# Conv mixer's tokens in phase order written by the norm ahead, and the channel norm's factor and bias moved into the silu

## The reference, cut to what matters

```python
def conformer_conv_mixer(h, w_in, b_in, dw, dw_b, ln_g, ln_b, w_out, b_out):
    a, gate = jnp.split(h @ w_in + b_in, 2, axis=-1)
    u = a * jax.nn.sigmoid(gate)                         # GLU, (B,S,D)
    u = depthwise_causal_conv(u, dw, width=31) + dw_b
    u = jax.nn.silu(layer_norm(u, ln_g, ln_b))           # over the channels
    return u @ w_out + b_out
for layer in range(2):
    h = h + 0.5 * swiglu_ffn(rms_norm(h, g), w_in, w_out)       # D_FF = 2816
    h = h + mixer[layer](rms_norm(h, g))
    h = h + memory_cross_attention(rms_norm(h, g), mem_n, wq, wkv, wo)
    h = h + 0.5 * swiglu_ffn(rms_norm(h, g), w_in, w_out)
y = rms_norm(h, final_norm)
```

## Time and profile before

| | us |
|---|---|
| median of 3 runs | 6055.49 (6054.27 to 6544.5) |
| profiled execution, device time | 6057.36 |
| its span on the slowest core (3) | 6055.7 |
| spans of the 8 cores | 6045.7 to 6055.7 |
| granted TensorE clock, mean | 0.986 to 0.987 |
| PE busy on that core | 5838.7 (96%) |
| DVE, ACT, POOL busy | 2989.5, 2245.4, 629.6 |

### The profile page before, as it was taken

The page is one execution under the profiler, slowest core; times in us unless marked ns, Lnnn a source line. Parts: engine busy times, 40 slices in busy tenths (PEclk is TensorE's granted clock), DMA queues, the critical chain, the costliest instruction groups (busy, mean ns, idle before and its releaser), DMA issues.

```text
span 6055.7 us, 91272 instructions; the slowest of 8 cores (6045.7 to 6055.7 us)
## 1 busy us (share of the span) xinstructions
PE 5838.7 (96%) x32113; PEld 2815.8 (46%) x32113; DVE 2989.5 (49%) x4244; ACT 2245.4 (37%) x3810; POOL 629.6 (10%) x700
## 2 busy tenths in 40 slices
PE   7999998999999998999989999899999999989999
PEld 3555554444444443444444445544444444445444
DVE  5444556643534523754364355564445344266435
ACT  4213888511311304641151158972123112266113
POOL 1100442000000000000000014400000000000000
PEclk9999999999999999999999999999999999989999
DMA  7665322322322022133352212224223202123221
GB/s 140 100 100 89 40 31 51 45 37 30 53 31 30 11 39 39 47 53 42 42 146 39 27 25 22 27 46 60 36 35 52 29 11 36 25 63 47 35 32 56
DMA packets 388456, 287.50 MB, mean 47 GB/s; under 512 B 111337, under 2 KB 344849, under 8 KB 385968
## 3 DMA queue, kind: packets, MB, share of 16 engines
q0 software_dynamic: 342192, 195.13, 25.2%
q1 hardware_dynamic: 45824, 86.55, 4.6%
HBM read 428.49 MB, written 33.55 MB: 76 GB/s over the span
## 4 chain that ended last, share of the span: by engine, by line
PE 91%; issue 2%; DVE 2%; ACT 2%; POOL 1%; DMA 1%; SPq 0%; DVEq 0%; ACTq 0%; POOLq 0%
PE ps L662 40%; PE ps L677 20%; PE ps L897 8%; PE ps L827 4%; PE ps L808 4%; PE ps L1050 3%; PE ps L577 2%; PE ps L1139 2%; PE ps L1002 2%; PE ps L925 2%; PE ps L1071 1%; PE ps L737 1%; PE ps L992 1%; DVE hn_tok L573 1%; PE ps L822 0%
## 5 line engine op out<-in xcount | busy, mean ns | idle before, releaser
L662 PE MATMUL ps<-arena 128*128 128x512 bf16 x11264 | 2487.5, 380 | 5.3 <-ACT arena L579 4.6
L662 PEld LDWEIGHTS ps<-arena 128*128 128x128 bf16 x11264 | 1098.8, 98 | 1314.2 <-issue 19.3
L664 ACT ACTIVATE arena<-ps 128x512 bf16<-128x512 f32 x704 | 419.7, 596 | 2584.3 <-PE ps L662 2573.6
L665 DVE TENSOR_TENSOR arena<-ps,arena 128x512 bf16<-128x512 f32 x704 | 486.8, 692 | 1768.2 <-PE ps L662 1751.1
L677 PE MATMUL ps<-arena 128*128 128x512 bf16 x5632 | 1248.5, 379 | 0.3 <-DVE h L679 0.3
L679 DVE SCALAR_TENSOR_TENSOR h<-ps,h 128x512 f32<-128x512 f32 x1536 | 1042.9, 690 | 213.1 <-PE ps L677 207.5
L677 PEld LDWEIGHTS ps<-arena 128*128 128x128 bf16 x5632 | 551.0, 98 | 663.9 <-issue 1.9
L897 PE MATMUL ps<-arena 128*128 128x512 bf16 x1024 | 468.0, 631 | 0.0
L604 POOL DMA_DIRECT2D arena<-ffn_w_in x176 | 154.6, 881 | 2426.7 <-PE ps L662 1729.1
L549 ACT ACTIVATE junk<-h 128x1024 bf16<-128x1024 f32 x288 | 303.8, 1055 | 233.7 <-DVE h L679 120.3
L1050 PE MATMUL ps<-arena 128*128 128x512 bf16 x1536 | 381.6, 387 | 0.0
(11 more groups left out here) (162 smaller groups left out, 4560.9 us busy)
## 6 DMA issues: line engine op xcount, KB each, us to landing
arena<-ffn_w_in POOLq DMA_DIRECT2D x176, 512.0 KB, 8.4
arena<-ffn_w_out POOLq DMA_DIRECT2D x88, 512.0 KB, 8.3
arena<-hgrn_w_in POOLq DMA_DIRECT2D x64, 256.0 KB, 5.4
y<-arena SPq DMA_DIRECT2D x32, 512.0 KB, 2.7
h<-x SPq DMA_DIRECT2D x20, 512.0 KB, 6.5
arena<-xattn_wkv POOLq DMA_DIRECT2D x16, 512.0 KB, 10.1
folded_a<-arena SPq DMA_DIRECT2D x16, 512.0 KB, 10.0
folded_v<-arena SPq DMA_DIRECT2D x16, 512.0 KB, 10.2
```

Of the source, the lines that this page charges most:

```text
L662: P.op("pe", lambda e, bb=bb, ga=ga, k=k, j=j: e.matmul(psb(bb), lhsT=wiv[:, ga, k, j * 128:(j + 1) * 128], rhs=hnT[:, k, blk * 512:(blk + ...
L664: P.op("act", lambda e, bg=bg, j=j: e.activation(out=sg[j].ap, in_=psb(bg), func=AF.Silu), reads=psk(bg), writes=sg[j].keys())
L665: P.op("dve", lambda e, bu=bu, j=j, q=q: e.tensor_tensor(out=actv[:, q, :], in0=psb(bu), in1=sg[j].ap, op=ALU.mult), reads=psk(bu) + sg[j] ...
```

## The change

- `norm_block` gets `phased`. For the conv mixer it multiplies each 128x128 piece of `hn_tok` with `phase`, a permuted identity, in place of the transpose: two PSUM banks and two ACT copies of 512 fp32 values a tile in place of one bank and one copy of 1024 bf16 values. `hnT` then lies in phase order, and `glu` reads 512 elements side by side.
- The channel norm's gain and bias are brought as columns into `vecs`, which has one value per partition. Where DVE made two passes and ACT a silu over each quarter, DVE makes one pass (minus mean, times 1/deviation, bf16 out), and the silu is taken as the results of the `spread` matmuls are copied out, all eight on ACT, with the factor and the bias of each channel. The broadcast loads of gain and bias are gone.
- At the end of a sequence `tail` also emits the norm of the next sequence's block `blk - 1`; the staging buffers of the final norm are four in place of two.
- The first FFN of each sequence begins with a pair of groups. In the first one `x` tiles 4 to 7 go through SP's queue, the second group's weights are loaded ahead of them, the loads of the folding steps wait for the last `x` tile ("tick"), and the steps lie at other packs.

```diff
+        phase = sb("phase", [128, 128], BF16)
...
+        P.op("pool", lambda e: e.tensor_copy(out=phase[:].rearrange("p (q s) -> p q s", q=4), in_=ident[:].rearrange("p (s q) -> p q s", q=4)), reads=["ident"], writes=["phase"])
...
-        def norm_block(blk, g, skip_rstd=False):
+        def norm_block(blk, g, skip_rstd=False, phased=False):
             if not skip_rstd:
                 block_rstd(blk)
             for tt in range(blk * 4, blk * 4 + 4):
                 s = tt % 2
                 P.op("dve", lambda e, tt=tt, s=s: e.scalar_tensor_tensor(out=hn_tok[:, s, :], in0=h[:, tt, :], scalar=stat[:, 2, tt:tt + 1], in1=gB[:, g, :], op0=ALU.mult, op1=ALU.mult),
                      reads=[("h", tt), ("rstd", blk), ("gB", g)], writes=[("hn_tok", s)])
+                if phased:
+                    part = hnT[:, :, blk * 512:(blk + 1) * 512].rearrange("p c (q f s) -> p c q f s", q=4, f=4)[:, :, :, tt % 4, :]
+                    for c0 in (0, 4):
+                        b = P.bank()
+                        for c in range(4):
+                            P.op("pe", lambda e, c=c, c0=c0, s=s, b=b: e.matmul(ps[:, P.place[b], c * 128:(c + 1) * 128], lhsT=hn_tok[:, s, (c0 + c) * 128:(c0 + c + 1) * 128], rhs=phase[:], start=True, stop=True),
+                                 reads=[("hn_tok", s), "phase"], writes=psk(b))
+                        P.op("act", lambda e, c0=c0, b=b, part=part: e.activation(out=part[:, c0:c0 + 4], in_=psb(b).rearrange("p (c q s) -> p c q s", c=4, q=4), func=AF.Copy), reads=psk(b), writes=hnT_keys(blk))
+                    continue
                 b = P.bank()
                 for c in range(KC):
                     P.op("pe", lambda e, c=c, s=s, b=b: e.transpose(out=psb16(b)[:, c * 128:(c + 1) * 128], in_=hn_tok[:, s, c * 128:(c + 1) * 128], identity=ident[:]),
                          reads=[("hn_tok", s), "ident"], writes=psk(b))
                 P.op("act", lambda e, tt=tt, b=b: e.activation(out=hnT[:, :, tt * 128:(tt + 1) * 128], in_=psb16(b).rearrange("p (c t) -> p c t", t=128), func=AF.Copy), reads=psk(b), writes=[k for c in range(KC) for k in hnT_buf.keys(c * T + tt * 128, c * T + (tt + 1) * 128)])
...
-        fin_stage = [ABuf(arena, ARENA_B - 8192 + i * 4096, D, F32) for i in range(2)]
+        fin_stage = [ABuf(arena, ARENA_B - 16384 + i * 4096, D, F32) for i in range(4)]
...
-                fs = fin_stage[fin_i[0] % 2]
+                fs = fin_stage[fin_i[0] % 4]
...
-            packs = [(0,)] + [(g, g + 1) for g in range(1, NG, 2)]
+            if which == 0 and layer == 0:
+                packs = [(0, 1), (2, 3), (4, 5), (6,), (7, 8), (9, 10)]
+            else:
+                packs = [(0,)] + [(g, g + 1) for g in range(1, NG, 2)]
             load_wi(0)
             if lead is not None:
-                lead(wi[base % NW].keys(0, KC * 256), wi[base % NW].keys(KC * 256, 2 * KC * 256), lambda: load_wo(0, [("landed", 0, 5)]))
+                load_wi(1)
+                lead(wi[base % NW].keys(0, KC * 256), wi[(base + 1) % NW].keys(0, KC * 256), lambda: load_wo(0, [("landed", 0, 5)]))
             else:
                 load_wo(0)
             for g in range(1, max(NW, NO)):
-                late = () if lead is None else [("landed", 0, (11, 13, 15, 15)[g - 1])]
-                if g < NW:
+                late = () if lead is None else [("landed", 0, (7, 13, 15, 15)[g - 1])]
+                if g < NW and (lead is None or g > 1):
                     load_wi(g, late)
                 if g < NO:
                     load_wo(g, late)
...
-                if middle is not None and i == 4:
+                if middle is not None and i == 2:
                     middle()
-                if steps and i >= 7:
+                if steps and i >= 4 and len(pack) == 2:
                     steps.pop(0)()
...
-                wload(wkv_[0], xa_wkv_d[l][:, hh * 256:(hh + 1) * 256].rearrange("(k p) n -> p k n", p=128), fw[0].keys())
-                wload(wkv_[1], xa_wq_d[l][:, hh * 256:(hh + 1) * 256].rearrange("(k p) n -> p k n", p=128), fw[1].keys())
+                wload(wkv_[0], xa_wkv_d[l][:, hh * 256:(hh + 1) * 256].rearrange("(k p) n -> p k n", p=128), fw[0].keys(), ["tick"])
+                wload(wkv_[1], xa_wq_d[l][:, hh * 256:(hh + 1) * 256].rearrange("(k p) n -> p k n", p=128), fw[1].keys(), ["tick"])
...
-            lnb = CV.take(D, F32)
...
                     ba = P.bank()
                     for (bb, a) in ((bg, 1), (ba, 0)):
                         for k in range(KC):
-                            P.op("pe", lambda e, bb=bb, a=a, k=k, v=v, blk=blk: e.matmul(psb(bb), lhsT=v[:, a, k, :], rhs=hnT[:, k, blk * 512:(blk + 1) * 512].rearrange("p (t q) -> p q t", q=4), start=(k == 0), stop=(k == KC - 1)),
+                            P.op("pe", lambda e, bb=bb, a=a, k=k, v=v, blk=blk: e.matmul(psb(bb), lhsT=v[:, a, k, :], rhs=hnT[:, k, blk * 512:(blk + 1) * 512], start=(k == 0), stop=(k == KC - 1)),
...
-            P.op("sp", lambda e: e.dma_start(out=lnb.ap, in_=cv_lnb_d[0].partition_broadcast(128)), writes=lnb.keys(), dma=True)
-            load_gain(ga, cv_lng_d[0])
             load_gain(gn, xa_norm_d[1])
             for b in range(NB):
...
                 for q in range(4):
                     a = b * 4 + q
                     uk = u2_keys(b, q, 0, D)
-                    P.op("dve", lambda e, b=b, q=q, a=a: e.scalar_tensor_tensor(out=u2v[:, b, q, :], in0=u2v[:, b, q, :], scalar=lst[:, 0, a:a + 1], in1=gB[:, ga, :], op0=ALU.subtract, op1=ALU.mult), reads=uk + [("lmean", b), ("gB", ga)], writes=uk)
-                    P.op("dve", lambda e, b=b, q=q, a=a: e.scalar_tensor_tensor(out=u2v[:, b, q, :], in0=u2v[:, b, q, :], scalar=lst[:, 5, a:a + 1], in1=lnb.ap, op0=ALU.mult, op1=ALU.add), reads=uk + lnb.keys() + [("lrs", b)], writes=uk)
                     yb = y_of(b, q)
-                    P.op("act", lambda e, b=b, q=q, yb=yb: e.activation(out=yb.ap, in_=u2v[:, b, q, :], func=AF.Silu), reads=uk, writes=yb.keys())
+                    P.op("dve", lambda e, b=b, q=q, a=a, yb=yb: e.tensor_scalar(out=yb.ap, in0=u2v[:, b, q, :], scalar1=lst[:, 0, a:a + 1], scalar2=lst[:, 5, a:a + 1], op0=ALU.subtract, op1=ALU.mult), reads=uk + [("lmean", b), ("lrs", b)], writes=yb.keys())
                 for c in range(KC):
                     bt = P.bank()
                     for q in range(4):
                         yb = y_of(b, q)
                         P.op("pe", lambda e, c=c, bt=bt, q=q, yb=yb: e.matmul(psb(bt), lhsT=yb.ap[:, c * 128:(c + 1) * 128], rhs=spread[:, q:q + 512], start=(q == 0), stop=(q == 3)), reads=yb.keys() + ["spread"], writes=psk(bt))
-                    if c % 2 == 0:
-                        P.op("act", lambda e, bt=bt, c=c, yTv=yTv: e.activation(out=yTv[:, c, :], in_=psb(bt), func=AF.Copy), reads=psk(bt) + ([("yT", b, 0)] if c else []), writes=[("yT", b, c)] + ([] if c else yk))
-                    else:
-                        P.op("dve", lambda e, bt=bt, c=c, yTv=yTv: e.tensor_copy(out=yTv[:, c, :], in_=psb(bt)), reads=psk(bt) + [("yT", b, 0)], writes=[("yT", b, c)])
+                    P.op("act", lambda e, bt=bt, c=c, yTv=yTv: e.activation(out=yTv[:, c, :], in_=psb(bt), func=AF.Silu, scale=vecs[:, V_LG, c:c + 1], bias=vecs[:, V_LO, c:c + 1]), reads=psk(bt) + [("vec", V_LG), ("vec", V_LO)] + ([("yT", b, 0)] if c else []), writes=[("yT", b, c)] + ([] if c else yk))
...
+        ahead = []
...
-                P.op("act", lambda e: e.activation(out=stat[0:1, 0, 18:19], in_=stat[0:1, 0, 0:1], func=AF.Copy), reads=[("ss", 0), ("h", 0)], writes=["tick"])
+                P.op("act", lambda e: e.activation(out=stat[0:1, 0, 18:19], in_=stat[0:1, 0, 0:1], func=AF.Copy), reads=[("ss", 0), ("h", 0), ("landed", 0, 15)], writes=["tick"])
...
+                    phased_at.add(len(seq_stages)) if layer == 1 else None
...
+                if sq_i + 1 < NSEQ:
+                    ahead.append(begin_norm(seq_stages[0][0]))
+
                 def tail(blk):
                     inner(blk)
+                    if sq_i + 1 < NSEQ and blk:
+                        norm_block(blk - 1, ahead[0])
...
-                g0 = begin_norm(seq_stages[0][0])
+                g0 = begin_norm(seq_stages[0][0]) if sq_i == 0 else ahead.pop()
                 def lead(k0, k1, then, g0=g0):
                     for tt in range(4, 8):
-                        load_x_tile(0, tt, "pool", k0 if tt < 6 else k1)
+                        load_x_tile(0, tt, "sp", k0)
                     norm_block(1, g0)
                     then()
                     for blk in range(2, NB):
                         for tt in range(blk * 4, blk * 4 + 4):
                             load_x_tile(0, tt, "pool", [("landed", 0, tt - 4)])
                         norm_block(blk, g0)
-                norm_block(0, g0)
-                if sq_i > 0:
-                    for blk in range(1, NB):
-                        norm_block(blk, g0)
+                norm_block(0 if sq_i == 0 else NB - 1, g0)
```

(11 more changed lines are left out.)

12 lines of the change are left out of this document (6 added, 6 removed).

## The result

The changed kernel took 5780.22, 5781.39, 6367.04 and 6465.86 us, with a median of 6074.22; the kernel before took 6054.27, 6055.49, 6332.73 and 6544.5, with a median of 6194.11 (the table of before has the three of them that were there then). In the two long runs of the changed kernel the cores of one die show a granted clock of 0.86 to 0.89 and the other die's cores spans of 5770 to 5783 us, so the comparison, and the times, ratios and means of the experiments, rest on runs and cores without this. The ratio to the kernel before is **0.9547 [0.9506, 0.9588]**, where the bracket is a 95% interval. The profiled execution took 5780.22 us, 277.1 less than the 6057.36 of before; the forecast's sum was 291.6.

What follows compares the result with a forecast made beforehand. PE was taken as the bound, with 91% of the chain of waits, losing time to slow glu matmuls and gaps. 241.6 - 4 + 20 + 22 + 12 = 291.6 us off 6057.4 gave 5765.8, stated as 5764 us; range 5736 to 5822.

Steps and rivals of the forecast that it cites:

- the median of the runs is 1.9 us below it: Last step: from the profiled execution's forecast of 5765.8 us to the median of the runs, 5764 us.
- Part 1: Conv mixer's glu: contiguous reads take a matmul from 452 to 216 ns, giving 241.6 us, less 4 us of new waits.
- for the first chunk 2 us a sequence: Glu's first chunk: the last block's norm has less glu to hide under; 4 us lost in all.
- Part 2: Norm in phase order: PE unchanged, ACT 5 us more in all, nothing on the path.
- Part 3: End of the conv mixer: one DVE pass and later silus give 10 us a sequence, 20 us; ends 4 and 30.
- PE's first output matmuls can pay 0 to 4 us for it: Conv mixer's end: eight silus in a row on ACT, 6.4 us, replace copies of 2.4 us and may delay PE.
- Rival 3: Seams fail through ACT's table order or norms holding up the last pack; sum 251 us, time 5805 us; chance 15%.
- Part 4: Change of sequence: norms emitted ahead and a paired first pack take back 22 of 28 us; ends 6 and 30.
- Part 5: Start: folding loads moved away and the second group's work put in PE's gap give 12 us; ends 3 and 18.
- the tiles land some 5 us earlier: Start: without the folding loads beside them the x tiles land sooner, while PE has 6.9 us of second-group matmuls.
- Sum: All terms together: 291.6 us off the profiled execution's 6057.4 us, which gives 5765.8 us.

Runs made afterwards that it cites:

- relay32: The changed kernel with the relayout issued as 32 DMAs of 16 channels in place of 16 of 32; 5932.63 us, one run.
- phase_alone: The kernel before with only the norm in phase order and glu's contiguous read; 5834.4 us in one run.
- rest_alone: The changed kernel with the plain norm and glu's read at a step of four set back; 6019.0 to 6022.4 us, ratio 0.9927.
- no_ahead: The changed kernel with the second sequence's norms emitted behind all final blocks, as before; 5808.96 us, one run.
- steps: The kernel before with eight read orders of the same 512 columns, one per conv mixer chunk; 216 to 918 ns a matmul.

## Why the prediction was right, and where not

The mechanism held for an execution of the kernel: 277 us against 291.6, and 5780 and 5781 us lie within 5736 to 5822. The stated time did not hold, since it stood for the median of the runs. By the steps:

- **From the sum to the median.** The step that failed is "the median of the runs is 1.9 us below it". The median of these four runs is 6074.22, 294.0 us above the profiled execution and outside the range, because two of them took 6367 and 6466 us. The sum took one execution's time for all and had no term for this, though a run of 6544.5 stood in the table of before. What makes an execution so long stays open.
- **Part 1.** The removed 241.6 measured 241.1 of PE's busy time. The new waits were put at 4 us, "for the first chunk 2 us a sequence", and came to about 9 (241.6 less the 232.6 of the account): 10.2 more in the first three chunks of both sequences, 1.3 less in the others. The sum took the steady queue of the earlier trace rows for the first chunks as well. The place of the relayout in a steady chunk was right to 0.2 us; relay32 showed that its slack is real and not large.
- **Part 2.** Zero was right: phase_alone's recurrences, conv end and change of sequence equal before's within 0.4 us. Its rest is 4.5 above, but rest_alone and no_ahead, from the same chip, have 2 to 4 more than the others too, and the kernel before took 8 us more there, so this seems to go with the chip.
- **Part 3.** 20 was forecast, 12.3 came. The step that failed is "PE's first output matmuls can pay 0 to 4 us for it": the gap's share was right (11.6 in one sequence, forecast 10.3 to 12.7), but PE pays nothing at the output matmuls. It pays 5.4 us a sequence at the attention's norm, where ACT's tables, 12 loads in place of 7, are changed between silu and root. Rival 3 named "silus behind ACT's table order" and gave it no price of its own. The DVE pass took 0.80 us, not the 1.28 that I took as its upper bound; the 32 spread matmuls took 9.03 us, not 6.92, at a granted clock of 0.78.
- **Part 4.** 22 was forecast, 27.6 came: nearly all of the 28 that I had counted, since the clock stayed up too. The reading that norms ahead and the pair are both needed held: either alone gives 8.5.
- **Part 5.** 12 was forecast, 6.5 came, less 2.7 in the recurrences. The step "the tiles land some 5 us earlier" and PE has the second group to do left out that this group's weights must land as early, over DMA engines without a free share: PE waits for them three times, 6.3 us.
- **Sum.** 5 + 8 + 5 + 3 less than forecast at parts 1, 3, 5 and the recurrences, 6 more at part 4: 15 us, and 14.5 are missing. That the sum came within 5% owes most to glu, which is 84% of it; among the small parts the forecast was off in both directions, by up to half of one.

## What to carry to other kernels

Look at the address pattern of a matmul's moving operand before its count: two kinds of matmul with the same tiles and a different mean in the page (379 and 631 ns) were 216 against 452 ns of pace. The mend here was to write the columns in the order in which they will be read, which the matrix product that transposes them did at no cost to be seen in the account. When an engine's work is moved to ACT, read which functions then alternate in its queue: here three table loads stood in 5 us. Where two waits follow each other at a seam, remove both: here one alone gave a third of the gain. Before a wait is put down to a load, look at where in time the load stands: the output weights come beside the last relayout, not beside the first.

## What the runs showed of the hardware

In steps a moving read of 512 bf16 columns took 227 ns at step 2, 452 at step 4, 900 and 918 at steps 8 and 16, and 229 in runs of four adjacent values, beside 216 contiguous; 1.76 ns for each 16-byte piece that it touches fits them. These times stayed the same at granted clocks of 1.00 and 0.50 (step 8) and of 1.00 and 0.81 (runs of 2), where contiguous columns went from 216 to 263. LDWEIGHTS took a mean of 115 ns beside the stepped read (before) and 98 beside the contiguous one (after). A change between Silu and Sqrt in ACT's queue showed a table load of 1.28 us each time. Splitting a relayout into twice as many DMAs of half the size, issued at 0.65 us each where it was 0.69, made it the bound of its loop, for 118 us over 16 chunks.
